# Gate rows of the modulation biased by VectorE on the way out of PSUM, and the turns of the modulation's pieces moved amid feature products

## What is computed

```python
mod = silu(c) @ w_ada + b_ada              # (9, 6 * 1024)
sh1, sc1, g1, sh2, sc2, g2 = split(mod, 6)
h = x * (1 + sc1) + sh1
mix = mixer_block(h, ...)                  # h @ w_in, three token mixers, @ w_out
x = layer_norm(ALPHA * x + g1 * mix)
h2 = x * (1 + sc2) + sh2
x = layer_norm(ALPHA * x + g2 * (relu(h2 @ w_up) ** 2 @ w_down))
```

## Time and profile before

| | |
|---|---|
| time, median of 3 runs | 2083.44 us (2082.27 to 2084.22) |
| the profiled execution, its own time | 2084.45 us |
| its span, first to last instruction | 2082.5 us |
| PE busy | 2040.3 us (98%) |
| DVE, POOL, ACT busy | 1435.5, 1436.7, 905.9 us |
| mean granted TensorE clock | 0.995 |
| chain that ended last | PE 74%, DVE 6% |

### The profile page before, as it was taken

How to read it: one execution, slowest core, us unless ns; L and a number is a source line. 1 busy time by engine, 2 the same in 40 slices (tenths; PEclk the granted TensorE clock), 3 DMA queues, 4 the chain that set the end, 5 groups by cost and what they waited for, 6 DMA issues and landing times.

```text
span 2082.5 us, 27969 instructions
## 1 busy us (share of the span) xinstructions
PE 2040.3 (98%) x10451; PEld 1711.9 (82%) x10451; DVE 1435.5 (69%) x1875; ACT 905.9 (43%) x1306; POOL 1436.7 (69%) x1101
## 2 busy tenths in 40 slices
PE   7999999999999999999999999999999989999996
PEld 5777888888997888888888888888888889999994
DVE  2564697695767455577887676888667757765686
ACT  2324223232223655455565454665455546444441
POOL 3346787864333677788888788888887856666672
PEclk9999999999999999999999999999999999999998
DMA  9896897963432554545445655445654633454341
GB/s 280 258 295 218 239 276 227 268 212 92 159 117 81 184 158 153 185 144 170 132 149 185 207 160 166 152 132 165 207 184 132 193 92 122 140 183 150 116 139 46
DMA packets 319952, 357.50 MB, mean 172 GB/s; under 512 B 12356, under 2 KB 251969, under 8 KB 319818
## 3 DMA queue, kind: packets, MB, share of 16 engines
q1 hardware_dynamic: 318954, 352.58, 54.0%
q10 hardware_dynamic: 864, 3.15, 0.5%
HBM read 321.22 MB, written 34.44 MB: 171 GB/s over the span
## 4 chain that ended last, share of the span: by engine, by line
PE 74%; DVE 6%; issue 0%; ACT 0%; DVEq 0%; ACTq 0%
PE ps L1215 24%; PE ps L1216 24%; PE ps L1217 24%; PE ps L1484 1%; PE ps L1558 1%; DVE htmp L1826 0%; DVE mix L1666 0%; DVE acc L1821 0%; DVE acc L1820 0%; PE ps L1355 0%; DVE st L1645 0%; DVE mix L1665 0%; DVE xt L2013 0%; PE ps L1336 0%; DVE xt L2011 0%
## 5 line engine op out<-in xcount | busy, mean ns | idle before, releaser
L915 POOL TENSOR_TENSOR w_hilo<-w_raw,w_hilo 128x512 fp32r<-128x512 f32 x890 | 1277.8, 1466 | 584.5 <-ACT w_hilo L996 584.1
L996 ACT ACTIVATE w_hilo<-w_raw 128x1024 fp32r<-128x1024 f32 x445 | 470.3, 1058 | 524.0 <-PE ps L1217 407.5
L1215 PE MATMUL ps<-hA,w_hilo 128*128 128x512 f32 (+1 forms) x1760 | 621.2, 353 | 6.9 <-ACT htmp L1082 6.1
L1216 PE MATMUL ps<-hA,w_hilo 128*128 128x512 f32 (+1 forms) x1760 | 619.3, 352 | 0.0
L1217 PE MATMUL ps<-hA,w_hilo 128*128 128x512 f32 (+1 forms) x1760 | 619.3, 352 | 0.0
L1215 PEld LDWEIGHTS ps<-hA,w_hilo 128*128 128x128 f32 x1760 | 331.3, 188 | 51.7 <-issue 8.5
L1216 PEld LDWEIGHTS ps<-hA,w_hilo 128*128 128x128 f32 x1760 | 331.4, 188 | 41.5
L1217 PEld LDWEIGHTS ps<-hA,w_hilo 128*128 128x128 f32 x1760 | 331.2, 188 | 41.2
L2048 DVE TENSOR_TENSOR acc<-acc,ps 128x512 f32<-128x512 f32 x270 | 177.6, 685 | 69.7 <-PE ps L1217 66.7
L1215 PE MATMUL ps<-w_hilo,hid_a 128*128 128x512 f32 x450 | 181.0, 402 | 0.4 <-ACT more_sums L1185 0.3
L1217 PE MATMUL ps<-w_hilo,hid_a 128*128 128x512 f32 x450 | 175.5, 390 | 0.0
(11 more groups left out here) (239 smaller groups left out, 2828.3 us busy)
## 6 DMA issues: line engine op xcount, KB each, us to landing
w_raw<-in_w_up SPq DMA_DIRECT2D x128, 512.0 KB, 4.1
w_raw<-w_mix SPq DMA_DIRECT2D x124, 512.0 KB, 3.3
w_raw<-in_w_down SPq DMA_DIRECT2D x97, 512.0 KB, 3.7
w_raw<-in_w_in SPq DMA_DIRECT2D x64, 512.0 KB, 4.9
xt<-in_w_ada SPq DMA_DIRECT2D x20, 1024.0 KB, 7.8
w_raw<-in_w_out SPq DMA_DIRECT2D x32, 512.0 KB, 4.4
xt<-x_norm SPq DMA_DIRECT2D x19, 512.0 KB, 5.8
xt<-in_w_down SPq DMA_DIRECT2D x36, 256.0 KB, 4.9
```

Of the source, the lines that this page charges most:

```text
L915: ins = pool.tensor_tensor(W[:, g % SLOTS, 1, cols], raw[:, g % RAW, cols], W[:, g % SLOTS, 0, cols], ALU.subtract)
L996: act.activation(W[:, g % SLOTS, 0, :], raw[:, g % RAW, :], ACT.Copy).then_inc(hi_done, 1)
L1215: pe.matmul(out, w_hi, x_hi, start=start, stop=False)
L1216: pe.matmul(out, w_hi, x_lo, start=False, stop=False)
```

## The change

The identity product goes, and with it the clearing of the bias rows' partitions and a wait of SP for the identity. VectorE adds the bias as it copies a gate's rows out of PSUM, and counts this on a semaphore of its own, `gate_T`; `ada_T` counts only shifts and scales. The turns leave their place behind the next product: those of the pieces that follow F(f - 1) are issued in the middle of F(f), after its fourth of eight k steps. The turn of piece 23 alone stays behind its product. The transposes behind it wait, for banks 0 and 1, for the last gate alone.

```diff
+def parts_turned(n):
+    return n if n <= ADA_FIRST else ADA_FIRST + (n - ADA_FIRST) // 2
...
         def ada_rows_out(u):
                 if is_gate(u):
-                    sp.wait_ge(ada_T, u + 1)
+                    sp.wait_ge(gate_T, gate_turn(u) + 1)
...
-            step(pool.memset(gs[:, 2 * ADA_COLS:], 0.0))
...
             def ada_turned(u):
+                if is_gate(u):
+                    return
                 act.wait_ge(ada_tr, u + 1)
-                if is_gate(u):
-                    act.activation(ada_rows(u), ps[0:1 + NB, bank, 0:ADA_COLS], ACT.Copy).then_inc(ada_T, 1)
-                    return
...
                     if s == 0 and SLAB_FM <= n < SLAB_O:
+                        for u in ada_pieces_after(n - SLAB_FM - 1) if n > SLAB_FM else []:
+                            ada_turned(u)
                         for u in ada_pieces_after(n - SLAB_FM):
                             ada_sums(u)
-                            if u > ADA_FIRST:
-                                ada_turned(u - 1)
...
             def ada_product(u):
-                if u >= 2:
-                    pe.wait_ge(ada_T, u - 1)
+                if u >= ADA_FIRST + 2 and is_gate(u):
+                    pe.wait_ge(gate_T, gate_turn(u))
+                elif u >= 2:
+                    pe.wait_ge(ada_T, parts_turned(u - 1))
...
                 if is_gate(u):
-                    pe.wait_ge(ada_rows_in[u // 2 % 2], 16 * (gate_turn(u) // 2 + 1))
                     o = ps[0:1 + NB, 1 + 2 * (u % 2), 0:ADA_COLS]
-                    pe.matmul(o, sel[:, :], ada_part(u), start=True, stop=False)
-                    ins = pe.matmul(o, ident[:, 0:1 + NB], ada_rows(u, P), start=False, stop=True)
+                    ins = pe.matmul(o, sel[:, :], ada_part(u), start=True, stop=True)
...
-            def fm_product(g, x, bank, nt):
+            def fm_product(g, x, bank, nt, turns):
...
                     for k in range(KD):
                         ins = mm3(...)
+                        if k == 3:
+                            for u in turns:
+                                ada_turn(u)
...
-                    if e == 1 and t == 0:
-                        pe.wait_ge(ada_T, N_ADA)
+                    if e == 1 and t:
+                        pe.wait_ge(ada_T, parts_turned(N_ADA))
+                    elif e == 1:
+                        pe.wait_ge(gate_T, gate_turn(N_ADA))
...
                     elif stage[0] == "A":
                         ada_product(stage[1])
-                        if stage[1] > ADA_FIRST:
-                            ada_turn(stage[1] - 1)
...
+            def gate_bias(u):
+                dve.wait_ge(ada_tr, u + 1)
+                dve.wait_ge(ada_rows_in[u // 2 % 2], 16 * (gate_turn(u) // 2 + 1))
+                dve.tensor_tensor(ada_rows(u), ps[0:1 + NB, 1 + 2 * (u % 2), 0:ADA_COLS], ada_rows(u),
+                                  ALU.add).then_inc(gate_T, 1)
...
                     if stage[0] == "F":
                         f = stage[1]
+                        for u in ada_pieces_after(f - 1) if first and f else []:
+                            if is_gate(u):
+                                gate_bias(u)
```

More of the change, by code:

```diff
@@ L430, in decoder_layer_kernel @@
         ada_T = sem("ada_T")
+        gate_T = sem("gate_T")
         ada_rows_in = [sem(f"ada_rows_in{i}") for i in range(2)]
@@ L548, in ada_part, with ada_rows @@
             return gs[:, ADA_COLS * (u % 2):ADA_COLS * (u % 2) + ADA_COLS]
-        def ada_rows(u, n=1 + NB):
-            return gs[0:n, ADA_COLS * (2 + u // 2 % 2):ADA_COLS * (2 + u // 2 % 2) + ADA_COLS]
+        def ada_rows(u):
+            return gs[0:1 + NB, ADA_COLS * (2 + u // 2 % 2):ADA_COLS * (2 + u // 2 % 2) + ADA_COLS]
         def hid(b, pair):
@@ L581, in ada_rows_load @@
                 if is_gate(u):
-                    if gate_turn(u) == 0:
-                        sp.wait_ge(s_ident, 1)
                     if gate_turn(u) >= 2:
@@ L1376, in mixer @@
                             pe.wait_ge(bias_kept, 1)
-                        fm_product(g0 + SLAB_FM + f, hA, fm_bank(f, nt, first), nt)
+                        fm_product(g0 + SLAB_FM + f, hA, fm_bank(f, nt, first), nt,
+                                   ada_pieces_after(f - 1) if first and f else [])
                     elif stage[0] == "B":
@@ L1623, in tables_turned @@
                                          None, ALU.add), s_biasT, 1)
+            def gate_bias(u):
[3 more added lines that the diff above has]
+                                  ALU.add).then_inc(gate_T, 1)
             def second_modulation():
-                dve.wait_ge(ada_T, N_ADA)
+                dve.wait_ge(ada_T, parts_turned(N_ADA))
                 sh2, sc2 = (modT[:, q * KD:q * KD + KD, :] for q in (SH2, SC2))
```

## The result

The changed kernel takes 2087.59 us in the median of 22 runs (2083.22 to 2090.56), the kernel before, on the same chip, 2084.22 (2082.27 to 2087.95, 22 runs). The ratio is 1.0013 [1.0007, 1.0019]. The prediction said 2082.9 with a range up to 2085.7: 0.5 less than the three runs of before that it had, where the measured median is 3.4 more than that of the 22. The runs of the changed kernel lie in two parts, and the difference can't be understood without them: 9 runs between 2083.2 and 2085.6 (median 2084.08, level with before), and 13 between 2087.0 and 2090.6 (median 2088.74). The runs of before, on all the chips used here, are above 2086 in 8 of 177.

A forecast was written before the change was run, and what follows sets the result against it. PE, busy for 98% of the span, was taken as the bound. +0.4 us at piece 16, -0.05 to piece 23 and -0.87 at the end gave -0.5: a median of 2082.9 us, range 2080.3 to 2085.7.

The forecast's parts named there:

- Pair amid a feature product: Two turns issued inside one feature product on PE add 1.15 us to it, bounds 0.85 and 1.45.
- Single gate: One gate's turn issued inside a feature product on PE adds 0.70 us, bounds 0.43 and 0.95.
- Product until the feature: A product with a feature product right behind it takes PE 0.95 us, bounds 0.86 and 1.00.
- Load 13 holds piece 13: First group: load 12 is issued 1.15 us later, load 13 lands at 93.3, and piece 13 starts then, not at 92.23.
- Load 15 holds piece 15: First group: load 15 lands at 105.4 and piece 15 starts then, after a wait of 1.6 us.
- The end: From piece 23 to the transposes PE takes 2.15 to 2.2 us instead of 3.07, so -0.87.
- VectorE's adds hide: VectorE's bias adds for the gates cost PE nothing; if late, each would cost up to 0.7 us.
- F4 starts at 106.35: Behind piece 15, F4 takes 5.71 + 1.15 us, so piece 16 starts at 113.2, 0.4 late.
- Behind it PE is nearly without idle time: After the first group, the sum of -0.5 us reaches the kernel's end whole.
- (a): Rival, chance 0.20: loads follow their issue, pieces 13 and 15 start when PE is ready; -3.2 us, 2080.2 us.
- (b): Rival, chance 0.15: breaks amid eleven feature products cost PE their high bound; +2.5 us in all, 2085.9 us.
- (c): Rival, chance 0.05: VectorE's add comes late to one or two gates behind F3 and F5; +0.7 to +1.4, about 2084 us.

The follow-up runs named there:

- i2: The changed kernel with 16 unread products of 16 columns on PE in its wait for the first loads; 2085.67 us, ratio 1.0005.
- g1: The changed kernel with the first weight mix loaded behind load 15 and five unread products ahead of the first transposes; 2084.51 us, ratio 1.0008.
- e3: The changed kernel with the two loads of the first weight mix issued behind load 15 instead of ahead of it; 2086.93 us, ratio 1.0013.
- f6: The kernel before with load 15 held back until VectorE has gated three tiles of the first group; 2083.86 us, ratio 1.0001.
- f7: The changed kernel without POOL's arithmetic on the mixes of slabs 24 to 47, loads and stores kept; 2083.53 us, ratio 1.0001.
- g3: The changed kernel with the 28 weight mixes spread over slabs 24 to 71 instead of 24 to 64; 2083.72 us, ratio 1.0000.
- h3: The changed kernel with the first mix's loads behind load 15 and the mixes spread over slabs 24 to 71; 2081.69 us, ratio 0.9992.
- f5: The kernel before with six unread products of 512 columns ahead of the first transposes; 2083.93 us, ratio 1.0004.
- g2: The kernel before with nine unread products of 512 columns ahead of the first transposes; 2084.4 us, ratio 1.0002.
- e1: The kernel before with the identity product taken out, turns in place, gate bias left out; 2085.28 us, ratio 1.0005.
- e2: The changed kernel with identity product and ACT's copy of the gate rows put back, so only the turns are moved; 2088.25 us, ratio 1.0020.
- e4: The changed kernel with eight unread products of 512 columns filling PE's wait ahead of piece 15; 2083.43 us, ratio 1.0001.
- h2: The kernel before without identity product and gate bias, each gate with a second product by sel of 16 columns; 2082.37 us, ratio 0.9991.

## Why the prediction was wrong, step by step

- *Pair amid a feature product*: 1.15 forecast. F1 runs from 73.63 to 80.53, 6.90 against 5.67: 1.23. *Single gate* 0.70: 115.63 to 122.09 is 6.46, so 0.79. *Single other* 0.62: 0.55 (123.09 to 129.31). *Product until the feature* 0.95: 1.00. From piece 16 to piece 23 this makes +0.46 (52.84 against 52.38) where -0.05 was forecast. The terms were near; breaks cost what rows 2 hinted, not nothing. The row behind VectorE's add, which the prediction calls a copy, is itself an add.
- *B's start, piece 10*: right (wait 1.00 instead of 1.3; 80.53 instead of 80.79).
- *Load 13 holds piece 13*: wrong. Load 12 was issued 0.89 later than before (81.74), and load 13 only 0.06, since it waits for product 11, which came no later. It landed 9.0 after its issue at 83.11, at 92.1, as before, and PE took it in its stride (91.19 + 0.9). This put piece 14 at 101.99, 0.96 sooner than forecast, and made the next wait longer by as much.
- *Load 15 holds piece 15*: right to 0.2 (105.18, 105.4 forecast), with a wait of 2.11 instead of 1.6.
- *The end*: -0.95 (2.12 against 3.07), -0.87 forecast. *VectorE's adds hide*: right, PE never waits for `gs` in the changed kernel.
- **First step that failed**: "F4 starts at 106.35 [...] and takes 5.71 + 1.15: piece 16 at 113.2". Time saved ahead of a load was taken to be lost at no charge. But in the profiled run the idle PE was followed by the lower clock, 1.5 us: piece 16 at 114.63. I had worked out a wait twice as long as any in the stretch and priced only its length. The Trainium skill, TensorE: Matmul & The Clock Gate, "What's actually happening", says that the throttled clock is the default and that activity releases it; this trace agrees, i2's doesn't show it.
- **Second, and larger**: "Behind it PE is nearly without idle time, so this reaches the end whole." PE had 0.68 us of idle time at the second group's transposes, and that was the sign to read: VectorE, without a break from 270 to 324, ended last there. The prediction lists PE's waits only up to 168.28. In the two upper runs that were profiled (changed, g1) this wait is 3 us and the clock falls behind it, about 4 us in all; the medians of the two parts lie 4.66 apart.

None of the rivals was it. (a) needed loads that follow, and e3 shows what it takes. (b) was near in the time (2085.9) and wrong in the mechanism: piece 14 was early, not late, and the breaks gave +0.5 behind piece 16, not +2.0. (c) asked for a wait at an even piece, and there is none. That the difference stays within 0.2% held. The lower part of the runs (2084.08, before 2084.22) lies close to the forecast of -0.5, but it is the better 9 of 22 runs by choice, and no trace shows by what it got there.

**Shown and not shown.** Shown: what the fall of the clock costs (9.45 against 7.90 us from piece 15 to 16); that load 15 is late by the queue's work ahead of it (e3, f6); that the late part comes from VectorE's work stretching beside POOL's mixes (f7, g3, and h3 against e3), and needs neither a later start (f5, g2) nor a fall in the first group (g1); that the moved turns cost what the identity product gave (e1, e2, e4). Not settled: what decides whether the clock falls behind a wait, and so whether filling the wait is what helped e4; why the changed kernel, e1, e3 and g1 draw the late part so often (13 of 22, 5, 8 and 5 of 11), but h2 and e4 hardly (0 and 1 of 11). With 11 runs each, the smaller of these differences may be chance. In the two late traces POOL waits only 2.9 and 2.7 us for the mixes' loads from 255 to 325, before 7.0; but e4 and i2, with no long wait of PE there, have 3.3 and 3.5. What sets these landings was not found.

## What to carry to other kernels

A saving ahead of a transfer that PE already waits for buys nothing there and can be worse than none: it makes the wait longer, and a longer wait can cost the clock; so move the transfer first (e3), then take the work out. Measure the parts of a change apart: here one part gave 3 us and the other took them. When PE is nearly full, look through the whole trace for the few places where another engine ends PE's wait, and ask whether that engine has slack: a saturated VectorE beside a busy POOL turned 0.7 us into 3.7, and the clock added to it. And a median hides two populations; list the runs.

## What the hardware showed that I had not expected

- The clock fell from 1.00 to 0.50 behind waits of 2.11 (changed kernel), 1.97 (f7) and 2.96 (second group of the changed kernel and of g1), and did not behind 1.77 (g3) and 2.57 (i2). The wait's length alone doesn't decide.
- VectorE's add of 512 columns with both inputs in SBUF takes 0.69 to 1.78 us, its cast 0.43 to 1.50 (profiles of before, changed, g1 and f7); with POOL's mixes out, the adds of the second group took 1197 ns in the mean instead of 1519 and the casts 521 instead of 950. With an input in PSUM the add took 0.69 every time.
- A load of 1 MB issued 2.05 us later let PE start 0.44 later (f6), with 0.22 of it in a later start of B.
